# Memory and x laid out by features in front of a two-block layer's first projections

## The reference

```python
mod = jax.nn.silu(c) @ w_ada[l] + b_ada[l]                 # c: (1, 1024), w_ada: (1024, 3072)
shift, scale, gate = jnp.split(mod, 3, axis=-1)
h = rms_norm(x, g_pre[l]) * (1.0 + scale[:, None, :]) + shift[:, None, :]
proj = h @ w_in[l]                                         # block 1: forgetting and sliding-window attention
...
mem_h = rms_norm_2(mem, mem_norm_g[l])                     # block 2's memory: (1, 256, 1024)
k, v = jnp.split(mem_h @ w_mem_kv, 2, axis=-1)             # keys get an rms norm of their own, per head
```

## Time and profile before

| | us |
|---|---|
| median of 3 runs | 1415.65 (1407.48 to 1416.24) |
| the profiled execution, its own time | 1415.13 |
| its span, first to last instruction | 1413.4 |
| PE busy | 1302.7 (92%) |
| DVE, ACT busy | 843.8 (60%), 594.8 (42%) |

### The profile page before, as it was taken

One profiled execution on the slowest core, in us unless ns is written; L12 is line 12 of the kernel. 1 busy time (PEld: TensorE's weight loads), 2 busy tenths in 40 slices (PEclk: granted clock), 3 DMA queues, 4 the chain that ended last, 5 costly groups with the idle time before them and its releaser, 6 DMA issues. The chain is left out here.

```text
span 1413.4 us, 17408 instructions
## 1 busy us (share of the span) xinstructions
PE 1302.7 (92%) x6598; PEld 1050.0 (74%) x6598; DVE 843.8 (60%) x1479; ACT 594.8 (42%) x1104; POOL 19.2 (1%) x36
## 2 busy tenths in 40 slices
PE   5989999988779599999999999899998899999998
PEld 5988777866559589777777776788776778588888
DVE  5775466355663432478787779478776666573341
ACT  6643344333432344555556555432554222462230
POOL 2000000000000000000000000000000000000001
PEclk9989999995759799999999999999999999999999
DMA  9965111110002312112211212323211222132221
GB/s 341 300 230 164 45 61 45 46 45 15 16 31 92 147 48 86 61 61 75 76 59 32 75 61 104 110 70 110 85 60 60 101 91 92 45 105 90 90 90 45
DMA packets 33027, 125.66 MB, mean 89 GB/s; under 512 B 3856, under 2 KB 4112, under 8 KB 32432
## 3 DMA queue, kind: packets, MB, share of 16 engines
q1 hardware_dynamic: 29520, 107.49, 23.3%
q0 software_dynamic: 3136, 16.75, 3.2%
q10 hardware_dynamic: 288, 0.31, 0.1%
HBM read 118.24 MB, written 6.29 MB: 88 GB/s over the span
## 5 line engine op out<-in xcount | busy, mean ns | idle before, releaser
L374 PE MATMUL bank<-hl,wh 128*128 128x512 f32 x880 | 367.7, 418 | 10.0 <-ACT th L926 4.7
L376 PE MATMUL bank<-hh,wh 128*128 128x512 f32 x880 | 348.1, 396 | 0.0
L375 PE MATMUL bank<-hh,wl 128*128 128x512 f32 x880 | 347.5, 395 | 0.0
L1446 DVE TENSOR_TENSOR wl<-raw,wh 128x1024 fp32r<-128x1024 f32 x179 | 214.4, 1222 | 118.8 <-ACT wh L898 117.2
L898 ACT ACTIVATE wh<-raw 128x1024 fp32r<-128x1024 f32 x179 | 184.2, 1053 | 210.6 <-PE bank L376 195.9
L374 PEld LDWEIGHTS bank<-hl,wh 128*128 128x128 f32 x880 | 168.6, 192 | 50.8 <-issue 15.8
L376 PEld LDWEIGHTS bank<-hh,wh 128*128 128x128 f32 x880 | 167.8, 191 | 37.3
L375 PEld LDWEIGHTS bank<-hh,wl 128*128 128x128 f32 x880 | 168.8, 192 | 35.0 <-issue 4.8
L1815 DVE SCALAR_TENSOR_TENSOR ca<-u,vt,ca 128x512 f32<-128x512 f32 x232 | 157.9, 745 | 0.0
L374 PE MATMUL bank<-wl,hh 128*128 128x256 f32 (+1 forms) x352 | 102.3, 291 | 5.0 <-DVE hl L2026 2.6
L375 PE MATMUL bank<-wh,hl 128*128 128x256 f32 (+1 forms) x352 | 100.7, 286 | 0.0
(11 more groups left out here) (263 smaller groups left out, 2052.1 us busy)
## 6 DMA issues: line engine op xcount, KB each, us to landing
raw<-in_chunks SPq DMA_DIRECT2D x203, 512.0 KB, 3.8
x<-in_x POOLq DMA_DIRECT2D x4, 512.0 KB, 10.5
mem_scratch<-kvm POOLq DMA_DIRECT2D x1, 2048.0 KB, 6.5
x<-in_x POOLq DMA_DIRECT2D x1, 2048.0 KB, 7.9
x_scratch<-x POOLq DMA_DIRECT2D x1, 2048.0 KB, 6.6
kvm<-mem_scratch POOLq DMA_DIRECT2D x1, 2048.0 KB, 8.1
x1r<-x_scratch POOLq DMA_DIRECT2D x1, 2048.0 KB, 8.7
out_x<-x1r POOLq DMA_DIRECT2D x8, 256.0 KB, 2.5
```

Of the source, the lines that this page charges most:

```text
L374: pe.matmul(o, a[0], b[1], start=start, stop=False, **kw)
L375: pe.matmul(o, a[1], b[0], start=False, stop=False, **kw)
L376: return pe.matmul(o, a[0], b[0], start=False, stop=stop, **kw)
L1446: dve.tensor_tensor(wl[:, w], raw[:, NRAW[nxt] % RAWS], wh[:, w].bitcast(F32), ALU.subtract)\
```

## The change

The host hands over x and the memory transposed (`x_t`, `mem_t`: 128 partitions x 8 chunks of features x tokens). The memory isn't normalised ahead of its products: hi and lo are taken from `memT` as loaded, and 1/rms is applied behind them. For the values (tokens on partitions) it is a factor of ACT's copy, now two copies a step; for the keys, whose own norm divides it out, only eps has to be right, which DVE does in `mem_mean`; the logarithm of all keys' means is now one ACT operation at the end. PE sums the squares of the memory in both layouts (`mem_ss` by matmuls on ones, `mem_rows` by one-column matmuls) between steps 0 and 1 of mk, and those of x (`x_ss`) between mk and mv. x is scaled in `xT` by DVE. There are no transposes in front. The tables, g_post, b_ada's gate part, b_fgate and positions are loaded behind the 16th piece of w_ada.

```diff
-            pe.wait_ge(s.nk_done, 2)
-            for g in range(4):
-                banks.open(pe, 2 + g, ("memT", g))
...
+                if h == 0:
+                    pe.wait_ge(s.const_in, 16)
+                    pe.wait_ge(s.mem_sq, 1)
+                    total("mem_ss", [msq[:, c, :] for c in range(C)], ones, MEM, 6)
+                    banks.open(pe, 5, "mem_rows")
+                    for tt in range(2):
+                        for c in range(C):
+                            ins = pe.matmul(ps[5][:, tt:tt + 1], msq[:, c, tt * P:tt * P + P], ones[:, 0:1],
+                                            start=c == 0, stop=c == C - 1)
+                    banks.close(ins, "mem_rows")
...
+            banks.open(pe, 6, "x_ss")
+            for c in range(C):
+                pe.wait_ge(s.x_sq, c + 1)
+                ins = pe.matmul(ps[6][:], ones, xsq[:, c, :], start=c == 0, stop=c == C - 1)
+            banks.close(ins, "x_ss")
             for g in range(4):
-                if g < 2:
-                    if g == 0:
-                        pe.wait_ge(s.xn_done, 4)
-                    to_features(xn, "xT", range(4 * g, 4 * g + 4))
@@ GpSimd's queue
+                pool.dma_start(xT[:, 2 * k:2 * k + 2, :], t["x_t"][:, 2 * k:2 * k + 2, :]).then_inc(s.x_in, 16)
...
+            pool.wait_ge(s.ada_used, 16)
             pool.dma_start(masks[:].rearrange("p a n -> p (a n)"), t["consts_b"][:, 0:2 * P]).then_inc(s.tables_in, 16)
...
@@ ScalarE
+            for c in range(C):
+                if c % 4 == 0:
+                    act.wait_ge(s.mem_in, 16 * 2)
+                act.activation(oh[:, c, 0:MEM], memT[:, c, :], ACT.Identity, scale=v("mem_g", c)).then_inc(s.h_hi, 1)
+                if c == 0:
+                    ahead(None, 1)
             ahead(None)
+            act.activation(msq[:], memT[:], ACT.Square).then_inc(s.mem_sq, 1)
...
+            banks.wait_full(act, "x_ss")
+            banks.empty(act.activation(rs, ps[6][:], ACT.Sqrt, scale=1.0 / D, bias=eps6), "x_ss")
...
+                act.wait_ge(s.mem_eps, 1)
+                for tt in range(2):
+                    ins = act.activation(vm[:, tt, MEM * g:MEM * g + MEM], ps[b][:, MEM * tt:MEM * tt + MEM], ACT.Copy,
+                                         scale=MEM_SS[:, tt:tt + 1])
...
+            act.activation(rsm[:], rsm[:], ACT.Ln).then_inc(s.eps_done, 1)
             act.activation(rsm[:], rsm[:], ACT.Exp, scale=-0.5).then_inc(s.rms_done, 1)
@@ VectorE
+            ahead(None, 1)
+            for c in range(C):
+                dve.wait_ge(s.h_hi, c + 1)
+                dve.scalar_tensor_tensor(oh[:, c, MEM:2 * MEM], memT[:, c, :], v("mem_g", c), oh[:, c, 0:MEM].bitcast(F32),
+                                         ALU.mult, ALU.subtract).then_inc(s.mem_lo, 1)
             ahead(None)
...
+            banks.wait_empty(dve, "x_ss")
+            then(dve.reciprocal(rs, rs))
+            for c in range(C):
+                dve.tensor_tensor(xT[:, c, :], xT[:, c, :], rs, ALU.mult).then_inc(s.xn_done, 1)
             for g in range(3):
+                if g == 0:
+                    mem_mean(3)
                 banks.wait_full(dve, ("mv", g, 0))
                 ahead(("mv", 2 * g + 1))
```

More of the change, by code:

```diff
@@ L103 @@
     "w_hi": "weight chunks whose hi is there", "w_lo": "and whose lo is", "ada_used": "pieces of w_ada multiplied and added",
-    "vec_done": "packed vectors scaled", "const_done": "constants converted", "eps_done": "eps there, then logarithms",
-    "c_tanh": "tanh(c / 2)", "small_sqrt": "roots of the mean squares of mem, then x", "lam_done": "lambda's sums, then exponentials",
+    "vec_done": "packed vectors scaled", "const_done": "constants converted", "eps_done": "eps there, then logarithms of the memory's mean squares",
+    "c_tanh": "tanh(c / 2)", "mem_lo": "and lo", "mem_sq": "the memory squared", "x_sq": "chunks of x squared", "mem_eps": "the memory's 1 / rms by rows",
+    "lam_done": "lambda's sums, then exponentials",
     "h_tmp": "chunks scaled and shifted", "dve_step": "VectorE's own steps", "sumsq": "rows of squares summed",
     "ms_done": "mean squares of block 1's tail", "sqrt_done": "their roots", "rms_done": "1 / rms taken on ScalarE",
-    "nk_done": "memory tiles normalised", "xn_done": "token tiles normalised (x, then x1)",
+    "xn_done": "token tiles normalised (x, then x1)",
     "kvm_ready": "chunks of the memory's keys normalised", "h_hi": "chunks of a block's input: hi", "h_lo": "lo",
@@ L992, in _ @@
                 ahead(("mk", 2 * h + 1))
+                if h > 0:
+                    x_squares_of(range(3 * h - 3, min(3 * h, 8)))
+            act.activation(warm2, eps6, ACT.Sqrt)
+            banks.wait_full(act, "mem_rows")
+            banks.empty(act.activation(MEM_SS, ps[5][:, 0:2], ACT.Sqrt, scale=1.0 / D, bias=eps6), "mem_rows")
+            banks.wait_full(act, "x_ss")
+            banks.empty(act.activation(rs, ps[6][:], ACT.Sqrt, scale=1.0 / D, bias=eps6), "x_ss")
             for g in range(4):
-                if g < 2:
-                    x_copies(g)
                 if g == 3:
@@ L1170, in _ @@
                     for n, tt in enumerate(tiles):
-                        if squares[0] > 6:
+                        if squares[0]:
                             act.wait_ge(s.sumsq, squares[0])
@@ L1478, in _ @@
             for h in range(4):
                 banks.wait_full(dve, ("mk", h, "k"))
-                ahead(("mk", 2 * h + 1))
-                if h == 0:
-                    dve.wait_ge(s.small_sqrt, 2)
-                    then(dve.reciprocal(X_SS, X_SS))
-                    for tt in range(T):
-                        dve.tensor_scalar(xn[:, tt, :], x[:, tt, :], X_SS[:, tt:tt + 1], None, ALU.mult).then_inc(s.xn_done, 1)
+                if h == 1:
+                    banks.wait_full(dve, "mem_ss")
+                    banks.empty(dve.tensor_scalar(mem_eps, ps[6][:, 0:MEM], 1e-6 / D, 1e-12, ALU.mult, ALU.add)
+                                , "mem_ss")
+                    banks.wait_empty(dve, "mem_ss")
@@ L1744, in small_root @@
                 then(dve.reciprocal(sums, sums))
-            squared = 6
+            squared = 0
             dve.wait_ge(s.v_lo, 5)
```

102 lines of the change are left out of this document (38 added, 64 removed).

## The result

The changed kernel takes 1429.7 us (median of 4 runs, 1427.93 to 1432.33); the kernel before took 1413.43 (4 runs, 1407.48 to 1416.24) beside it. The ratio is 1.0117, with an interval of 1.0089 to 1.0145: slower by 1.2%. The forecast was 1425.7 with a range of 1414 to 1433; the likeliest case had 1421 to 1430.

A forecast was written before the change was run, and what follows sets the result against it. It took PE, busy without gaps from 28.2 to 69.5 us, as the bound, so added PE work counts in full. +9.0 us at "mod" and +1.1 for rsm gave +10.1, so 1425.7 us, range 1414 to 1433.

The forecast's parts named there:

- Start at 12.4: First matmul of mk: PE starts at 12.4 instead of 19.55 us, a gain of 7.1.
- The wait for the squares, 2.3: Ahead of mem_ss: PE waits 2.3 us because ACT squares the memory only behind chunks 2 and 3.
- mem_ss 3.5, mem_rows 4.5, step 1 +1.6: PE between steps 0 and 1 of mk: new sums take 3.5 and 4.5 us, a fallen clock adds 1.6 to step 1.
- DVE's scaling in the ring: Between chunks 11 and 12: reciprocal 3.2 and eight multiplications 4.9 us delay lo 12, and so the 16th piece to 81.1.
- "mod" waits 3.8, +9.0: At "mod": PE waits 3.8 us for pieces instead of 2.4, and "mod" starts 9.0 us later than before.
- "mod" and mv 3, 14.08: Between the start of "mod" and fa: these keep their 14.08 us, so fa starts at 95.2 instead of 86.14.
- Tables, 0: POOL's queue: loading 1.8 MB of tables later gains nothing and costs 0, at most 4 us.
- rsm +1.1: Chain to fa's bank: the keys' logarithms in one late ACT operation and extra copies cost 1.1 us.
- A: Rival for the head: the load ring, not PE, bounds it, so late tables make the kernel faster, 1410; chance 0.10.
- B: Rival: sparse matmuls and wide reciprocal are cheap, clock stays at 2.4 GHz through mem_rows, reciprocal 0.6 us: 1420.3; chance 0.12.
- C: Rival: late tables collide with pieces 16 and 17 (+4), plus a cold step 1 and 4.3 us reciprocal: 1432; chance 0.13.
- D: Rival for the start: PE doesn't start earlier, as first chunk or packed vectors come late; at most 3 us, within the range.

The follow-up runs named there:

- e5: The changed kernel measured again as it is, in the second group: 1427.48 us, ratio 1.0113 against the kernel before.
- e2: The changed kernel with the four lambda loads and the sinks load also behind the 16th piece of w_ada: 1424.14 us, ratio 1.0074.
- e1: The changed kernel with ACT's squares of the memory ahead of the hi of chunks 2 and 3: 1421.15 us, ratio 1.0052.
- e6: The changed kernel with DVE's eight multiplications of xT spread over chunks 12 to 17 instead of all ahead of chunk 12: 1429.55 us, ratio 1.0118.
- e8: The changed kernel with e1, e2 and e7 together, x's squares, sum and reciprocal earlier, and multiplications spread from chunk 8 on: 1415.74 us, ratio 1.0015.
- e12: e8 with x's squares right behind ACT's copies of chunks 2 and 3 and both reciprocals at step 2: 1418.16 us, ratio 1.0035.
- e11: The kernel before with tables, broadcast vectors, lambda and sinks all behind the 16th piece of w_ada: 1410.98 us, ratio 0.9984.
- e3: The kernel before with only the changed kernel's POOL queue (lambda and sinks behind x, tables late): 1409.38 us, ratio 0.9969.
- e4: The kernel before with the x part of the change alone, memory and tables as they were: 1419.4 us, ratio 1.0037.
- e7: The changed kernel with squares and ones as fp32r, mem_rows' matmuls two columns wide: 1427.69 us, ratio 1.0092.
- e9: The changed kernel with its x part undone (x by rows, transposes back), memory part and late tables kept: 1428.82 us, ratio 1.0111.
- e10: The changed kernel with POOL's queue in the order of the kernel before (tables early, right behind x): 1424.38 us, ratio 1.0086.

## Why the prediction was right, and what in it was not

The sign and the place were right, and the time lies in the range: +10.1 us forecast, +12.8 in the span and 16.3 between the medians beside each other (13.2 in e5). The loss sits in the first 115 us, and behind them everything shifts (fa's bank by 13.56). Several of the signs named for "right" did not come: step 1 ended at 42.38 (36 to 39.5 forecast), "mod" started at 84.52 (79 to 83), and the clock fell ahead of the sparse matmuls and not in or behind them. Step by step:

- **Start at 12.4.** It was 13.99. The first chunk took 9.4 us from issue to its copy (ACT starts it at 11.06), where I had 8.1 from the earlier trace rows; that is 1.4 of the 1.6 us. Step 0 then went faster than forecast (7.76 us, not 8.3).
- **The wait for the squares, 2.3.** It was 5.70: the term that was mis-sized. I let chunk 3 land at 20.0 from the earlier trace rows; it was copied at 24.45. Its slot was free at 17.76 and not 16.6, and from there it took 6.7 us and not 3.4. I had read the diff's POOL part as "the tables go" and missed that the five small loads move in front of them. e2 sends them late and has 3.6 us back at chunk 3, with the 3.4 us from slot to copy that I had assumed (17.42 to 20.84); e1 removes the whole wait. ACT's order, `ahead(None)` before the square, was named right.
- **mem_ss 3.5, mem_rows 4.5, step 1 +1.6.** Measured 5.61, 3.49 and +0.07: 9.6 forecast, 9.2 measured. The sum came out by luck: the clock did fall, but in the wait ahead and not behind the sparse matmuls, so that mem_ss paid for it and the other two did not. In e1, where no wait was, it fell where I had put it, and step 1 took 8.32.
- **x_ss 6.9, ends at 59.2.** 6.46, ends at 62.92; the 3.7 us are those of the wait and the start.
- **DVE's scaling in the ring.** 3.2 forecast for the reciprocal, 3.33 measured; 4.9 and 4.91 for the multiplications. The Trainium skill ("VectorE: DVE Perf Modes", First, the fixed hardware budget) led to an estimate of 4.3; the row of 3.33 decides against it, and the growth from one to four columns in the earlier trace rows was the better guide. x_ss to the 16th piece was 21.9 forecast and 21.54 measured. Yet the reason was largely wrong. I wrote that it "stands in the ring between chunks 11 and 12" and that its time is therefore paid. e6 spreads the multiplications and gains 0.6 us, and the whole block can cost 2.0 ahead of lo 12. What is paid is PE's: chunk 12 needs the slot of chunk 8, and "mod" follows the end of mv 0 by 14.9 to 17.4 us in every kernel of the table but e8 and e12. The right time came from a chain that was paid only at its end, by luck, because the two had nearly the same length here.
- **"mod" waits 3.8, +9.0.** 2.93 and +12.46.
- **"mod" and mv 3, 14.08.** 12.57 (84.52 to 97.09), 1.5 cheaper: "mod" 5.28 and mv 3 7.29, before 5.58 and 8.50. It came to nothing, since DVE's chain to fa's bank starts at "mod" too: PE waited 5.03 us there and not 2.42.
- **Tables, 0.** Right for the changed kernel: POOL issues them from 84.76 on, nobody waits for `bcast_in`. In the kernel before late tables are worth 0 to 4 us.
- **rsm +1.1.** 0.68 of wait and about 0.25 for two more copies.

Of the rivals, A (the ring bounds the head) fell for this change: DMA share in mk went from 0.92 to 0.57 without a gain, and PE had no gap from 33 to 56 us. Late tables in the kernel before brought 1.1 (e11) and 5.8 us (e3) between medians. The ring did bind where PE was faster: in e4's mk, and in e8 and e12. B was right in half: mem_rows and step 1 did run at the full clock here (3.49 and 5.83), but the reciprocal is 3.33 and mem_ss paid the fall of the clock. C's collision didn't come (16th piece to `modc` 7.24 us, before 7.15). D is in the 1.6 us of the start.

So the expected gain, PE's earlier start by 5.56 us, was eaten by a wait of 5.70 before a single product more was done, and PE's new matmuls, 15.56 us (5.61 + 3.49 + 6.46) against 3.34 of transposes between the products that went, came on top. e8, in which they are cheap and the first wait is gone, has none of the loss and no gain: 1415.74 us against 1414.28, with PE waiting for chunks. Whether another order could turn the earlier start into time is not shown.

Open stays why step 1 runs in part at the lower clock in some kernels (e1, e6, e7, e9, e10: 7.8 to 8.3 us) and not in others (changed, e2, e5, e8, e12: 5.8). The length of the wait ahead doesn't sort them: none in e1 and e8, 4 to 5 us in e7 and e9, 5.9 in e5. Open too is whether the 5.8 us of e3's median are real: its marks have none of them.

## What to carry to other kernels

An earlier start is worth nothing by itself here: count what stands between it and the point from which the rest of the kernel follows, here the end of mv 0, whose product frees the slot of the next chunk. Work that moves from ACT and DVE to an engine that is 100% busy in the stretch costs in full, and in fp32 it cost two to four times the fp32r price here. When a diff reorders a queue, price what moves to the front as well as what leaves it, and look for waits that an instruction inherits from its place in a queue and not from its data: one line earlier on ACT was worth 4 us at the marks and 9 between medians.
